# The input projection of layer 1's attention with split operands, its rows handed over tile by tile, and the rotation of the keys on GpSimd

## What is computed

```python
h = modulate(rmsnorm(x, norm_mix[1]), shift, scale)    # 512 latent rows, 256 context rows
z = h @ w_in                                            # 1024 x 672
cq  = z[..., :384]            # latent rows alone are used
ckv = z[..., 384:640]
kr  = z[..., 640:]            # 32 columns, one key part for all heads
q  = rmsnorm(cq, q_norm) @ w_uq
kv = rmsnorm(ckv, kv_norm) @ w_ukv
kr = apply_rope(kr, cos, sin)                           # latent rows alone
```

## Time and profile before

| | us |
|---|---|
| median of 3 runs (lowest, highest) | 1917.29 (1916.35, 1918.03) |
| time of the profiled execution | 1916.38 |
| its span, first to last instruction | 1914.6 |
| mean granted TensorE clock in it | 0.947 of full |
| PE busy in the span | 1655.4 |
| DVE, ACT, POOL busy in the span | 653.2, 514.2, 202.5 |

### The profile page before, as it was taken

The page is one execution under the profiler, slowest core; times in us unless marked ns, Lnnn a source line. Parts: engine busy times, 40 slices in busy tenths (PEclk is TensorE's granted clock), DMA queues, the critical chain, the costliest instruction groups (busy, mean ns, idle before and its releaser), DMA issues.

```text
span 1914.6 us, 22850 instructions
## 1 busy us (share of the span) xinstructions
PE 1655.4 (86%) x9277; PEld 816.8 (43%) x9277; DVE 653.2 (34%) x1359; ACT 514.2 (27%) x873; POOL 202.5 (11%) x199
## 2 busy tenths in 40 slices
PE   5999969579999999999879989988849978777874
PEld 2677748323333333333245757757613322222221
DVE  4666664611212212122234655655441101011111
ACT  5678763201101111011141534535300000000001
POOL 1000010000000000000000413413000100000000
PEclk8999989789999999999979899899969999999998
DMA  9454441899999999998741000002589999999997
GB/s 364 165 199 157 176 176 78 338 374 409 410 396 403 404 390 406 382 403 322 254 169 66 1 0 0 0 0 119 209 338 405 398 398 414 400 413 398 412 408 290
DMA packets 92084, 528.61 MB, mean 276 GB/s; under 512 B 11875, under 2 KB 20176, under 8 KB 36448
## 3 DMA queue, kind: packets, MB, share of 16 engines
q1 hardware_dynamic: 80704, 489.84, 63.6%
q0 software_dynamic: 11296, 37.58, 6.9%
HBM read 504.21 MB, written 23.17 MB: 275 GB/s over the span
## 4 chain that ended last, share of the span: by engine, by line
PE 61%; SPq 20%; ACT 6%; DVE 5%; DMA 5%; issue 3%; ACTq 0%; DVEq 0%; POOLq 0%
SPq L463 20%; PE wide L737 14%; PE duo L777 6%; PE wide L650 6%; PE wide L745 6%; PE turned L516 6%; PE wide L590 5%; PE duo L787 3%; PE duo L958 2%; PE wide L935 2%; PE duo L880 2%; DMA sb_ring<-ada_w 2%; DMA sb_ring_x<-moe_w_down 1%; PE duo L899 1%; PE wide L845 1%
## 5 line engine op out<-in xcount | busy, mean ns | idle before, releaser
L737 PE MATMUL wide<-sb_ring_x,sb_xT 128*64 128x512 f32 x1136 | 271.5, 623 | 33.6 <-DMA sb_ring_x<-moe_w_up 32.5
L737 PE MATMUL wide<-sb_ring,sb_xT 128*64 128x512 f32 x912 | 212.3, 607 | 29.1 <-DMA sb_ring<-moe_w_up 27.4
L1565 DVE TENSOR_TENSOR sb_hid<-wide,sb_sg 128x512 f32<-128x512 f32 x32 | 22.1, 692 | 616.6 <-ACT sb_sg L1174 310.9
L1174 ACT ACTIVATE sb_sg<-wide 128x512 f32<-128x512 f32 x32 | 19.2, 599 | 668.2 <-PE wide L745 340.8
L737 PEld LDWEIGHTS wide<-sb_ring_x,sb_xT 128*64 128x64 f32 x1136 | 79.0, 142 | 212.6 <-issue 140.5
L777 PE MATMUL duo<-sb_ring_x,sb_hidT 128*64 128x512 f32 x592 | 138.3, 600 | 10.3 <-DMA sb_ring_x<-moe_w_down 10.1
L1865 POOL DMA_INDIRECT stream<-sb_ye,sb_idx_t x30 | 43.1, 1435 | 901.6 <-DVE sb_ye L1588 901.6
L737 PEld LDWEIGHTS wide<-sb_ring,sb_xT 128*64 128x64 f32 x912 | 62.1, 138 | 166.0 <-issue 108.4
L1877 POOL TENSOR_TENSOR sb_prob<-sb_prob,sb_asum 128x768 f32<-128x768 f32 x64 | 93.9, 1467 | 261.3 <-DVE sb_asum L1741 261.3
L1580 DVE SCALAR_TENSOR_TENSOR sb_ye<-duo,sb_gate_t,sb_gffn 64x512 f32<-64x512 f32 x30 | 22.3, 742 | 203.9 <-PE duo L787 103.6
L1194 ACT ACTIVATE sb_ye<-duo 64x512 f32<-64x512 f32 x30 | 17.9, 596 | 271.1 <-PE duo L787 146.8
(11 more groups left out here) (336 smaller groups left out, 2517.4 us busy)
## 6 DMA issues: line engine op xcount, KB each, us to landing
sb_ring_x<-moe_w_up SPq DMA_DIRECT2D x142, 1024.0 KB, 15.0
sb_ring<-moe_w_up SPq DMA_DIRECT2D x114, 1024.0 KB, 18.9
sb_ring_x<-moe_w_down SPq DMA_DIRECT2D x80, 1024.0 KB, 18.0
sb_ring<-moe_w_down SPq DMA_DIRECT2D x48, 1024.0 KB, 16.1
sb_ring<-ada_w SPq DMA_DIRECT2D x40, 1024.0 KB, 6.8
sb_ring<-lru_w_in SPq DMA_DIRECT2D x8, 1024.0 KB, 9.1
sb_ring_x<-ada_w SPq DMA_DIRECT2D x8, 1024.0 KB, 7.5
sb_ring<-lru_w_out SPq DMA_DIRECT2D x4, 1024.0 KB, 6.6
```

What stands on the lines that cost most here:

```text
L737: ins = mm(wide[n * CAPL:(n + 1) * CAPL, s, :], xT[:, k, 0:CAPL], w[:, at:at + BANK], start=k == 0, stop=k == KD - 1)
```

## The change

There are four edits. First, `w_in` and the rows are split: ACT copies each weight block to a new tile `mla_hi`, DVE writes the rest over the block in the ring, and for each row tile ACT copies `hT` to `hT2_hi` (which lies where `xn` was) and DVE writes the rest over `hT` (`hT2_lo`). Second, each product is made of three matmuls in float32r. Third, the order on the engines: ACT and DVE prepare two tiles (three norms), then take the product of tile t, the norm of tile t + 3 and the rows of tile t + 2 in turn, and PE turns tile t + 2 right behind the matmuls of tile t. Fourth, DVE raises `s_cqn` after the key copy, and the rotation runs on GpSimd.

```diff
+        def mla_w(k):
+            ...
+            return ring[:, slot, cols_], mla_hi[:, k, :], ring_r[:, slot, cols_]
+        def mla_lhs(t):
+            tile = slice(t * P, (t + 1) * P)
+            return hT2[:, :, tile], hT2_hi[:, t, :].rearrange("p (k n) -> p k n", k=KD), hT2_lo[:, :, tile]
 # PE
-                    pe.wait_ge(s_hTa, N0[2] + t + 1)
-                    pe.wait_ge(s_hTd, N0[2] + t + 1)
+                    pe.wait_ge(s_hlo, MLA_L0 + t + 1)
                     for k in range(KD):
-                        if t < TLT:
-                            mm(wide[:, b, 0:QL], lhs, mla_w(k)[:, 0:QL], start=k == 0, stop=k == KD - 1)
-                        ins = mm(wide[:, b + 1, 0:MZ - QL], lhs, mla_w(k)[:, QL:MZ], start=k == 0, stop=k == KD - 1)
+                        if t == 0:
+                            pe.wait_ge(s_wlo, MLA_W0 + k + 1)
+                        for i, (lhs, w) in enumerate(((lhs_hi, w_hi), (lhs_lo, w_hi), (lhs_hi, w_lo))):
+                            if t < TLT:
+                                mm(wide[:, b, 0:QL], lhs[:, k, :], w[:, 0:QL], **edge)
+                            ins = mm(wide[:, b + 1, 0:MZ - QL], lhs[:, k, :], w[:, QL:MZ], **edge)
-                    for t in {0: (2,), 1: range(3, TT)}.get(step, ()):
-                        turn_tile(2, t)
+                    if step + 2 < TT:
+                        turn_tile(2, step + 2)
 # ACT
             act.wait_ge(s_modev, 6)
-            norm(2)
+            for k in range(KD):
+                act.wait_ge(landed[slot], 16 * n)
+                fn(hi, w, ACT.Copy).then_inc(s_whi, 1)
+            def mla_rows(t):
+                modulate(2, t)
+                act.wait_ge(s_hTa, N0[2] + t + 1)
+                act.wait_ge(s_hTd, N0[2] + t + 1)
+                fn(hi, h, ACT.Copy).then_inc(s_hhi, 1)
+            for t in range(3):
+                squares(2, t)
+                if t >= 1:
+                    mla_rows(t - 1)
             for t in range(TT):
                 ...
+                if t + 3 < TT:
+                    squares(2, t + 3)
+                if t + 2 < TT:
+                    mla_rows(t + 2)
 # DVE (its weights, its mla_rows and its loop in the same shape)
+                v.tensor_tensor(lo, w, hi.bitcast(F32), ALU.subtract).then_inc(s_wlo, 1)
+                v.tensor_tensor(lo, h, hi.bitcast(F32), ALU.subtract).then_inc(s_hlo, 1)
-                        ins, rest = turn_angles(krr[:, t:t + 1, :], kraw[:, t % 2:t % 2 + 1, :], 1, t)
+                        v.tensor_copy(kraw[:, t % 2, :], kr).then_inc(s_cqn, 1)
 # GpSimd, ahead of its attention loop
+            for t in range(TLT):
+                pool.wait_ge(s_cqn, t + 1)
+                _, rest = turn_angles(g_, krr[:, t:t + 1, :], kraw[:, t % 2:t % 2 + 1, :], 1, t, s_krr)
+                for o, a_, b_, op in rest:
+                    g_.tensor_tensor(o, a_, b_, op).then_inc(s_krr, 1)
```

More of the change, by code:

```diff
@@ L396, in out_lhs, with turn_angles @@
             return Y[:, :, tile], Y_hi[:, t % 2], Y_lo[:, :, tile]
-        W0 = [2 * KD, 3 * KD]
-        L0 = [KD, KD + TT]
+        W0 = [2 * KD, 4 * KD]
+        L0 = [KD, KD + 2 * TT]
+        def mla_w(k):
+            j = [n for n, (a, b) in enumerate(MLA_K) if a <= k < b][0]
+            cols_ = slice((k - MLA_K[j][0]) * MZ, (k - MLA_K[j][0] + 1) * MZ)
+            slot = place["mla_in", j][0]
+            return ring[:, slot, cols_], mla_hi[:, k, :], ring_r[:, slot, cols_]
+        def turn_angles(eng, dst, src, n, t, done=None):
+            x1 = src.rearrange("p n (a h f) -> p n a h f", a=2, h=2)[:, :, :, 0, :]
+            x2 = src.rearrange("p n (a h f) -> p n a h f", a=2, h=2)[:, :, :, 1, :]
+            o1 = dst.rearrange("p n (a h f) -> p n a h f", a=2, h=2)[:, :, :, 0, :]
+            o2 = dst.rearrange("p n (a h f) -> p n a h f", a=2, h=2)[:, :, :, 1, :]
+            cos, sin = [ropes[:, t, i, :].rearrange("p (a f) -> p a f", a=2).unsqueeze(1).to_broadcast([P, n, 2, FQ]) for i in range(2)]
+            tmp = [rtmp[:, j, 0:n * 2 * FQ].rearrange("p (n a f) -> p n a f", n=n, a=2) for j in range(4)]
+            for j, (a_, b_) in enumerate(((x1, cos), (x2, sin), (x1, sin), (x2, cos))):
+                ins = eng.tensor_tensor(tmp[j], a_, b_, ALU.mult)
+                if done:
+                    ins.then_inc(done, 1)
+            return ins, [(o1, tmp[0], tmp[1], ALU.subtract), (o2, tmp[2], tmp[3], ALU.add)]
+        def mla_lhs(t):
+            tile = slice(t * P, (t + 1) * P)
+            return hT2[:, :, tile], hT2_hi[:, t, :].rearrange("p (k n) -> p k n", k=KD), hT2_lo[:, :, tile]
+        MLA_W0, MLA_L0 = 3 * KD, KD + TT
         def mod_bank(i):
@@ L819, in _ @@
             turn_tile(2, 1)
-            hT = stages[2]["hT"]
-            for j in range(3):
-                arrived(("mla_in", j))
-            def mla_w(k):
-                j = [n for n, (a, b) in enumerate(MLA_K) if a <= k < b][0]
-                return ring_at(("mla_in", j))[:, (k - MLA_K[j][0]) * MZ:(k - MLA_K[j][0] + 1) * MZ]
             for step in range(TT + 1):
@@ L1010, in modulate @@
                 ins.then_inc(s_hTa, 1)
-            def norm(s):
-                n = stages[s]["n"]
-                for step in range(n + 1):
-                    if step < n:
-                        squares(s, step)
-                    if step >= 1:
-                        modulate(s, step - 1)
             act.wait_ge(s_const, NCONST)
@@ L1294, in modulate @@
                 ins.then_inc(s_hTd, 1)
-            def norm(s):
-                n = stages[s]["n"]
-                for step in range(n + 1):
-                    if step < n:
-                        normed_tile(s, step)
-                    if step >= 1:
-                        modulate(s, step - 1)
             def ada_read(i):
```

57 lines of the change are left out of this document (36 added, 21 removed).

## The result

| | before | after |
|---|---|---|
| median of 5 runs (lowest, highest) | 1917.29 (1916.35, 1919.11) | 1909.48 (1905.61, 1911.36) |
| profiled execution: time, span | 1916.38, 1914.6 | 1911.36, 1909.6 |
| mean granted TensorE clock in it | 0.947 | 0.944 |

The ratio is 0.9956, 95% interval 0.9943 to 0.9968: 7.8 us faster, where 14 were forecast, and above the range's upper end of 1908.0. The profiled execution is the slowest of the five.

A forecast was written before the change was run, and what follows sets the result against it. PE was taken to bound the stage ahead of the attention loop; terms of -1.3, -1.7, -10.6, -4.1, -1.7, -0.75, -0.75 against +1.1, +1.8, +2.8, +1.3 summed to -13.9 us, forecasting 1903.0, range 1900 to 1908.

The forecast's parts named there:

- the clock term: Tile 5, last context tile: the granted clock may fall in PE's idle time just ahead; 1.3 us more was taken.
- the gap: PE between the matmuls of tiles 1 and 2: only turns remain, 1.4 us instead of 12.0, 10.6 less.
- the new wait: PE ahead of tile 5, the last context tile: stands 3.6 us at tile 3's cqn turn until DVE has written cqT.
- The clock at the new wait: PE's idle 3.6 us ahead of tile 5: a fallen clock costs at most 2.6 us, nothing if it holds; 1.3 taken.
- The Trainium skill's rule: PE's wait ahead of tile 5 brings back the half clock: all of tile 5 slow, forecast 1904.3 instead of 1903.0.
- Runs of this kernel lie within 0.1% of each other: Whole kernel's run times: on this spread, 0.2% (3.8 us) was taken as what can be told from no change.
- noise of 1: Allowance of 1 us for run-to-run noise in the low end of the forecast range, 1900.
- All of it stays: Behind the attention loop's start, through layer 1's expert stream: engines wait for each other, so the whole 13.9 us gain is kept.
- Rival (d): Layer 1's expert stream: bound by something outside, so the gain is given back later, 1917; chance 0.05.
- (b): Handovers of tiles 1 to 3: GpSimd's small rotation instructions hold up DVE, 3 to 6 us, 1908; chance 0.11.
- (c): Split matmuls of 288 columns on PE: weight loads keep them from 0.13 us each, 8.2 us more, 1911; chance 0.06.
- (e): Every tile's handover: rows come from ACT and DVE later than PE wants them, making it slower, 1920; chance 0.02.

The follow-up runs named there:

- the second profile: The changed kernel, unaltered, run and profiled once more on another occasion; measured 1904.83 us, ratio 0.9929 to the kernel before.
- the order alone: The changed kernel with its order by tile and GpSimd rotation, but float32 products and nothing split; measured 1906.50 us, ratio 0.9944 to the kernel before.
- the version with the rows further ahead: The changed kernel with four norms and three rows prepared ahead of product 0 and earlier turns on PE; measured 1902.12 and 1900.02 us.
- the cut kernel: A kernel without layer 1's choice of experts, experts and their weights; 1408.51 us for the kernel before, 1392.86 to 1399.23 for the changed one.

## Why the prediction missed

**What held, term by term.** In the first profile the start is 1.15 us later (forecast +1.1; +1.4 over five profiles), tile 0 takes 9.53 (9.3), tiles 1 to 3 7.4 to 7.5, the gap is 1.34 (1.4), the copy and the subtraction are 1.06 and 1.23, the new wait 3.42 (3.6), and the 5.33 us of ACT's weight copies are hidden. The stage without the clock term was forecast at -15.2; where the clock held it is 76.52, 76.58 and 76.51, against 91.18 of before: -14.6.

**Where the recorded miss lies.** The profiled pair is 5.0 us apart, where 13.9 were forecast. Of the 8.9 us between, the stage has 1.8 (12.1 shorter), the stretch from the loop's start to the first expert weights 0.7, layer 0 ahead of the stage 1.9 (945.64 and 943.77) and the stretch from the first expert weights to the end 4.6 (593.8 and 589.2). The first two are for the most part the step below, the stage's with 1.4 of its 1.8. The last two are chance as far as is known: two profiles of the kernel before differ by 0.95 and 3.2 us in them.

**The step of the working that failed** is "The clock at the new wait": "so I take the middle, 1.3 more", with "at most 2.6 more". There is no middle. With the same wait to 0.01 us the clock falls in one execution and holds in the next. Where it falls the stage is 79.14 and 79.41, 2.7 us longer; and it goes on costing outside the term, 6.2 to 6.4 instead of 5.39 us for the loop's first eight matmuls. From the loop's start to the first expert weights of layer 1 the profiles have 291.03 and 291.80 where it fell and 290.66 where it held, another 0.4 to 1.1. The sum was worked out with only the matmuls of tile 5 in it, and the turn ahead of them and the start of the loop were left out: a fall costs some 3 to 4 us, not 2.6. The Trainium skill's rule, TensorE: Matmul & The Clock Gate, HAM oscillation, that was set against the middle, described the profile of the recorded block: 18 of tile 5's 24 matmuls were slow there. In the second profile, with the same 3.41 us of idle PE, none was, so here the rule gives what can happen, not what does.

**The second step**, and the larger one in the recorded block, is the noise. "Runs of this kernel lie within 0.1% of each other" rested on three runs. Over 79 executions of the kernel before they reach from 1914.1 to 1924.7, with a standard deviation of 2.2; the changed kernel's 17 have 3.4. A clock that falls or holds probably adds to it, but isn't all of it, for the order alone, with a wait of 0.31 us there, has 3.7 in six executions. A median of five such runs is good to some 2 us, so a range with "noise of 1" could not hold it. The mean of all 17 is 1907.6, 10.8 ± 0.9 below before's 1918.4, and that is the best number for the change: the recorded block is low by 3 and the forecast of 14 high by 3. Half of each measured price, -14.6 and -11.9 and the 0.4 to 1.1 behind it, would have been -13; of the 2 us from there to 10.8 the cause is open.

**"All of it stays"** is not decided. With the experts left out the mean gain is 13.3 ± 0.8; whole it is 10.8 ± 0.9. Against a part given back stands the version with the rows further ahead, which by its means is 16.5 faster cut and 16.9 whole, and the experts' stretch itself: from the first expert weights to the end the profiles of before have 589.2 and 592.4 us and the three of the changed kernel 593.8, 592.0 and 590.6. Rival (d) is not shown. What else takes 1 to 2 us in single executions, in layer 0 (943.6 to 946.6 us until the stage, for every kernel here) and around the attention loop, stays open, and so does what makes the longer executions of the order alone, apart from what lies outside their spans.

**The other rivals.** (b) is refuted as a price: DVE's norm, which does run beside GpSimd's rotation, takes 0.76 where it took 0.75, and with the rotation on DVE the cut kernel is 2.3 slower. It is GpSimd that is held up: in the first profile its first four instructions take 1.24 to 1.32 us for tiles 0 to 2, beside the norm, and 0.76 for tile 3, where DVE evicts instead. With the rows further ahead DVE evicts beside the rotation of tiles 1 and 2 too, and it takes 0.76 there. Nobody waits for it, so it costs nothing here. The subtraction, the one with two SBUF inputs, starts only when the rotation has ended, so the rule of the Trainium skill that stood beside this rival (GPSIMD Engine Reference, Specifications) was not put to the test. (c) is refuted: the matmuls of 288 columns start 0.13 apart. (e) is refuted: no wait for `sb_hT_lo` behind tile 0.

**Where the gain comes from.** The working gave the four gaps and tiles to order and splits together. Taken apart, the order is worth 12.1 us of the stage (79.04) and the splits in the old order 0.7 (90.49). On top of the order the splits bring 2.5 us of the stage where the clock holds and nothing where it falls: they save some 6 us of matmuls (tiles 1 to 3 go from 9.04 to 7.47, the context tiles from 3.9 to 3.3), but start 1.3 later and make the new wait, 3.4 instead of 0.3. In the mean of the cut kernels they bring 0.7 (1395.8 and 1395.1; by the spans nothing), in the whole ones nothing that shows (1906.2 and 1907.6). The profiles say where the 2.5 go: the order alone has the clock at 1.00 at the loop's start, where the whole change has 0.50, and is 3.0 us shorter from there to the expert weights (287.63 and 290.66). So its forecast, half a microsecond off, was met by some luck: the stage is 12.1 shorter, not 11.3, and the clock at the loop's start was in no sum.

## What to carry to other kernels

Where a faster product empties an engine's queue just ahead of a wait, the wait and the clock behind it are the price: here 6 us of saved matmuls came to 2.5 us of the stage or to nothing, until the rows were prepared one tile further ahead, which gave 3 (cut) to 6 (whole) more. Treat a clock that may fall as two outcomes with their own chances, price all that runs behind the wait, and never take a mean of the two. Where two kernels are compared by their times, look at the granted clock outside the changed stage as well: here it differed at the start of the attention loop by 3 us. And look at ten runs, not three, before saying what a microsecond is.
